# Odd layer's block inverses: PE turns in place of the products that make the transposes, blocks laid home by token tile

## The reference

```python
def rwkv7_scan(r, logw, k, v, kk, a, s0):
    def step(s, inp):
        r_t, lw_t, k_t, v_t, kk_t, a_t = inp
        sa = jnp.einsum('bhvk,bhk->bhv', s, -kk_t)
        s = (s * jnp.exp(lw_t)[:, :, None, :] + sa[..., None] * (kk_t * a_t)[:, :, None, :]
             + v_t[..., None] * k_t[:, :, None, :])
        return s, jnp.einsum('bhvk,bhk->bhv', s, r_t)
```

## Time and profile before

| | us |
|---|---|
| median of 3 runs | 1579.1 (1577.63 to 1582.22) |
| profiled execution | 1576.2, its span 1574.3 |
| PE busy in the span | 1487.2 (94%) |
| DVE, ACT busy | 545.6 (35%), 296.3 (19%) |
| odd layer's blocks 0 to 7, z of block 0 to solve of block 7 | 604.02 to 792.21 |
| experts, to the end | the last 700 or so |

### The profile page before, as it was taken

One profiled execution on the slowest core, in us unless ns is written; L12 is line 12 of the kernel. 1 busy time (PEld: TensorE's weight loads), 2 busy tenths in 40 slices (PEclk: granted clock), 3 DMA queues, 4 the chain that ended last, 5 costly groups with the idle time before them and its releaser, 6 DMA issues.

```text
span 1574.3 us, 62507 instructions
## 1 busy us (share of the span) xinstructions
PE 1487.2 (94%) x28005; PEld 1323.4 (84%) x28005; DVE 545.6 (35%) x1410; ACT 296.3 (19%) x817; POOL 16.4 (1%) x32
## 2 busy tenths in 40 slices
PE   5999888999998999999887999999999999999995
PEld 3888477999546787888866999999999999999995
DVE  1463435666636344666843301010101011010102
ACT  2112423010102432444324101010101010010101
POOL 0100000000000000000000000000000000000000
PEclk9999998999998999999998999999999999999998
DMA  9722676444448144000132799999999999999993
GB/s 391 292 82 100 250 300 270 161 174 181 182 167 314 40 162 150 6 8 8 33 151 81 300 417 379 416 386 418 384 412 409 387 419 380 418 376 417 376 418 131
DMA packets 72895, 407.07 MB, mean 259 GB/s; under 512 B 10514, under 2 KB 10948, under 8 KB 35908
## 3 DMA queue, kind: packets, MB, share of 16 engines
q1 hardware_dynamic: 68176, 398.92, 64.0%
q0 software_dynamic: 1184, 3.41, 0.7%
q10 hardware_dynamic: 3412, 2.93, 0.6%
HBM read 403.31 MB, written 1.92 MB: 257 GB/s over the span
## 4 chain that ended last, share of the span: by engine, by line
PE 37%; PEld 10%; DVE 1%; ACT 1%; issue 1%; PEldq 0%; DVEq 0%; POOL 0%; ACTq 0%
PE bank L1466 20%; PE bank L1486 10%; PEld bank L1466 7%; PEld bank L1486 3%; PE bank L644 2%; PE bank L1448 1%; PE bank L1432 1%; PE bank L1442 0%; PEld bank L1432 0%; PE bank L709 0%; PE bank L1267 0%; PEld bank L1448 0%; DVE w L2036 0%; DVE w L2675 0%; PE bank L1290 0%
## 5 line engine op out<-in xcount | busy, mean ns | idle before, releaser
L1466 PE MATMUL bank<-w,ring 128*64 128x86 f32 x11264 | 452.6, 237 | 1.1 <-ACT w L1959 0.6
L1466 PEld LDWEIGHTS bank<-w,ring 128*64 128x64 f32 x11264 | 432.4, 136 | 9.7 <-issue 8.8
L1486 PE MATMUL bank<-w,ring 128*64 128x86 f32 x5632 | 238.7, 237 | 0.0
L2860 DVE TENSOR_TENSOR w<-w,bank 128x86 f32<-128x86 f32 x176 | 43.1, 245 | 549.0 <-PE bank L1466 541.6
L1486 PEld LDWEIGHTS bank<-w,ring 128*64 128x64 f32 x5632 | 220.8, 137 | 0.0
L1971 ACT ACTIVATE w<-bank 128x86 f32<-128x86 f32 x176 | 42.8, 243 | 572.4 <-PE bank L1466 572.4
L641 PE MATMUL bank<-w,ring 128*128 128x256 f32 x256 | 59.1, 394 | 4.3 <-DVE w L2454 3.7
L641 PEld LDWEIGHTS bank<-w,ring 128*128 128x128 f32 x256 | 50.5, 198 | 13.0 <-DVE w L2454 4.0
L644 PE MATMUL bank<-ring,w 128*128 128x256 f32 x256 | 56.0, 380 | 1.9 <-DVE w L2036 1.9
L644 PEld LDWEIGHTS bank<-ring,w 128*128 128x128 f32 x256 | 48.4, 190 | 8.8 <-DVE w L2036 2.3
L667 PE MATMUL bank<-ring,ct 128*32 128x256 f32 x768 | 47.0, 396 | 2.4 <-ACT ct L1569 2.1
(11 more groups left out here) (437 smaller groups left out, 1795.9 us busy)
## 6 DMA issues: line engine op xcount, KB each, us to landing
ring<-in_moe_gu SPq DMA_DIRECT2D x176, 1024.0 KB, 8.5
ring<-in_moe_w_down SPq DMA_DIRECT2D x176, 512.0 KB, 8.6
ring<-in_ada_w SPq DMA_DIRECT2D x48, 1024.0 KB, 5.0
ring<-in_ev_w_in SPq DMA_DIRECT2D x11, 1024.0 KB, 26.6
ring<-in_ffn_w_gate SPq DMA_DIRECT2D x11, 1024.0 KB, 7.9
ring<-in_ffn_w_up SPq DMA_DIRECT2D x11, 1024.0 KB, 5.2
ring<-in_ffn_w_down SPq DMA_DIRECT2D x11, 1024.0 KB, 6.4
ring<-in_ev_w_out SPq DMA_DIRECT2D x4, 1024.0 KB, 11.0
```

Source lines behind the costliest of these rows:

```text
L1466: ins = [mm(b[hp, 0:CAP], w[:, k, hp], XG[:, k, :], start=k == 0, stop=k == KC - 1, skip_group_check=True) for hp in HALVES]
L1486: ins = [mm(bank[4 + c // 4][hp, (c % 4) * CAP:(c % 4 + 1) * CAP], w[:, c * P + hp.start:c * P + hp.stop], HIDU[:, t % 2, :], start=t == 0 ...
L2860: v.tensor_tensor(HIDU[:, t % 2, :], SILU[:, t % 2, :], bank[2 + t % 2][:, 0:CAP], ALU.mult).then_inc(sem("hid"), 1)
```

## The change

The second part of xp goes at levels 1 to 4. In its place PE turns the new X, four turns of 128x128 into bank 2 (turned_x), and ACT copies the needed columns into IP (take_turned). At level 5 the product stays (last_p), with DVE's masked copy behind it (last_wider). turned_start is four turns as well. For a turn to give what is wanted, the blocks are laid so that the two token tiles lie on the two halves of the partitions (P, z) or the two heads do (X): z writes half j // 2 and reads both, new_x reads half j // 2 and writes both. wider makes four copies of half the size. right_side, solve and carry follow the new layout, and take_right is one copy instead of two. The eight PSUM banks become one tensor with views.

The order changes on each engine: on PE t4(i, 2), t4(i, 3), turned_keys, t4(i + 1, 0) and right_side come earlier, last_states now stands behind right_side and waits for ACT's copies of level 5; on DVE masked(i, 2) stands ahead of wider(i, 1); on ACT take_turned stands ahead of each take_z, the decays are split.

```diff
-        bank = [ctx.enter_context(nc.psum_tensor(f"bank{i}", [P, 512], F32)) for i in range(8)]
+        banks = ctx.enter_context(nc.psum_tensor("banks", [P, 4096], F32))
+        bank = [banks[:, i * 512:(i + 1) * 512] for i in range(8)]
...
-        IP = [tiles4(HTf[:, 512 * k:512 * k + 512]) for k in range(2)]
-        IX, IZ = tiles4(HTf[:, 1024:1536]), tiles4(HTf[:, 1536:2048])
-        GS = tiles4(GBf[:, 0:512])
+        IP = [HTf[:, 512 * k:512 * k + 512].rearrange("p (d a h n) -> p d a h n", d=2, a=2, h=2) for k in range(2)]
+        IX, IZ = HTf[:, 1024:1536].rearrange("p (d a b n) -> p d a b n", d=2, a=2, b=2), tiles4(HTf[:, 1536:2048])
+        GS = GBf[:, 0:512].rearrange("p (r d a n) -> p r d a n", r=2, d=2, a=2)
...
+        def four(lo):
+
+            return banks[:, lo * 512:(lo + 2) * 512].rearrange("p (g n) -> p g n", g=4)
+
+        def state_bank(i):
+
+            return bank[1 if i + 1 < KC else 7]
...
-                    pe.wait_ge(sem("zc"), 10 * i - 1 + d)
-                for j in range(4):
-                    for hp in HALVES:
-                        at = home(d, hp)
-                        ins = mm(bank[2 + d][hp, j * DH:(j + 1) * DH], IP[i % 2][at, d, j, :], ID2[at, :], start=True, stop=True)
-                        if j == 3:
-                            ins.then_inc(sem("z"), 1)
+                    pe.wait_ge(sem("zc"), 18 * i)
+                for a in range(2):
+                    at = (2 * d + a) * P
+                    ins = tr(bank[3][:, at:at + P], IP[i % 2][:, d, a, :, :].rearrange("p h n -> p (h n)"), ident)
+                ins.then_inc(sem("z"), 2)
 
             def z(i, lv):
 
                 if lv == 1:
                     pe.wait_ge(sem("x0"), 2 * i + 2)
                     pe.wait_ge(sem("m4"), 4 * i + 2)
-                    if i:
-                        pe.wait_ge(sem("inv"), 10 * i)
+                    if i >= 2:
+                        pe.wait_ge(sem("so"), i - 1)
                 else:
                     pe.wait_ge(sem("ix"), 8 * i + 2 * (lv - 1))
                 for j in range(4):
+                    to = HALVES[j // 2]
                     for d in range(2):
-                        for hp in HALVES:
-                            ins = mm(z_bank(lv, d)[home(d, hp), j * DH:(j + 1) * DH], M4[i % 2][0][hp, j, 0, queries(d, hp), :],
-                                     IX[hp, d, j, :],
+                        at = (j % 2) * 256 + d * DH
+                        for h, hp in enumerate(HALVES):
+                            ins = mm(bank[h][to, at:at + DH], M4[i % 2][0][hp, j, 0, queries(d, hp), :],
+                                     IX[hp, d, j % 2, j // 2, :],
                                      start=True, stop=True)
                             if j == 3:
                                 ins.then_inc(sem("z"), 1)
 
-            def xp(i, lv):
-                pe.wait_ge(sem("zc"), 10 * i + 2 * lv)
-                if lv > 1:
-                    pe.wait_ge(sem("inv"), 10 * i + 2 * (lv - 1))
-                if lv < 5:
-                    for j in range(4):
-                        for d in range(2):
-                            for hp in HALVES:
-                                at = home(d, hp)
-                                ins = mm(z_bank(lv + 1, d)[hp, j * DH:(j + 1) * DH], IP[i % 2][at, d, j, :], IZ[at, d, j, :],
+            def new_x(i, lv):
+
+                if lv == 1:
+                    pe.wait_ge(sem("zc"), 18 * i + 2)
+                    if i:
+                        pe.wait_ge(sem("inv"), 2 * i)
+                else:
+                    pe.wait_ge(sem("zc"), 18 * i + 4 * lv - 2)
+                for j in range(4):
+                    st, a = j // 2, j % 2
+                    for d in range(2):
+                        at = a * 256 + d * DH
+                        for h, hp in enumerate(HALVES):
+                            ins = mm(bank[2 + st][hp, at:at + DH], IP[i % 2][HALVES[st], d, a, h, :], IZ[HALVES[st], d, 2 * h + a, :],
+                                     start=True, stop=True)
+                            if j == 3:
+                                ins.then_inc(sem("nx"), 1)
+
+            def turned_x(i, lv):
+
+                pe.wait_ge(sem("ix"), 8 * i + 2 * lv)
+                for d in range(2):
+                    for a in range(2):
+                        at = (2 * d + a) * P
+                        ins = tr(bank[2][:, at:at + P], IX[:, d, a, :, :].rearrange("p b n -> p (b n)"), ident)
+                    ins.then_inc(sem("np"), 1)
+
+            def last_p(i):
+
+                pe.wait_ge(sem("zc"), 18 * i + 18)
+                for d in range(2):
+                    for a in range(2):
+                        for h in range(2):
+                            at = (4 * d + 2 * a + h) * DH
+                            for to in HALVES:
+                                ins = mm(bank[2][to, at:at + DH], IZ[to, d, 2 * h + a, :], IP[i % 2][to, d, a, h, :],
                                          start=True, stop=True)
-                                if j == 3:
-                                    ins.then_inc(sem("nx"), 1)
-                for d in range(2):
-                    for j in range(4):
-                        for hp in HALVES:
-                            ins = mm(z_bank(lv, 0)[hp, (4 * d + j) * DH:(4 * d + j + 1) * DH], IZ[hp, d, j, :], IP[i % 2][hp, d, j, :],
-                                     start=True, stop=True)
-                            if d == 1 and j == 3:
-                                ins.then_inc(sem("np"), 1)
+                                if (d, a, h) == (1, 1, 1):
+                                    ins.then_inc(sem("np"), 1)
...
             def last_states(i):
                 pe.wait_ge(sem("trk"), i + 1)
-                pe.wait_ge(sem("y_copy"), i + 1)
+                if i + 1 < KC:
+                    pe.wait_ge(sem("zc"), 18 * (i + 2))
+                else:
+                    pe.wait_ge(sem("y_copy"), i + 1)
                 for h in range(2):
                     for m in range(2):
...
-                    t4(i, 2)
-                xp(i, 1)
+                    t4(i, 3)
+                new_x(i, 1)
                 if i:
                     carry(i - 1)
+                turned_x(i, 1)
                 z(i, 2)
                 if i == 0:
                     half_v(3, 1)
                 else:
-                    t4(i, 3)
-                xp(i, 2)
+                    turned_keys(i - 1)
+                new_x(i, 2)
                 if i:
                     solve(i - 1, 1)
+                turned_x(i, 2)
                 z(i, 3)
                 if i == 0:
                     pe.wait_ge(sem("v_copied"), 3)
                     ada_part(11, 0)
-                else:
-                    turned_keys(i - 1)
-                xp(i, 3)
+                if more:
+                    t4(i + 1, 0)
+                new_x(i, 3)
                 if i:
                     outputs(i - 1)
+                turned_x(i, 3)
                 z(i, 4)
                 if i == 0:
                     ada_part(11, 1)
                 if more:
-                    t4(i + 1, 0)
-                xp(i, 4)
-                z(i, 5)
-                if more:
                     t4(i + 1, 1)
-                xp(i, 5)
+                new_x(i, 4)
                 if i == 0:
                     turn_mods(11)
                 else:
+                    right_side(i)
+                turned_x(i, 4)
+                z(i, 5)
+                if i:
                     last_states(i - 1)
-                right_side(i)
+                last_p(i)
+                if i == 0:
+                    right_side(0)
                 if more:
                     for d in range(2):
                         turned_start(i + 1, d)
+                    t4(i + 1, 2)
                 solve(i, 0)
...
-                    act.wait_ge(sem("z"), 24 * i + 4 * lv + 2 * d + 2)
-                    A(sided(IZ[:, d, :, :], lv, d), sided(z_bank(lv, d)[:, 0:256].rearrange("p (j n) -> p j n", j=4), lv, d),
+                    act.wait_ge(sem("z"), 24 * i + 4 * lv + 4)
+                    A(sided(IZ[:, d, :, :], lv, d), sided(four(0)[:, :, d * DH:(d + 1) * DH], lv, d), ACT.Copy).then_inc(sem("zc"), 1)
+
+            def take_turned(i, lv):
+                for d in range(2):
+                    act.wait_ge(sem("np"), 10 * i + 2 * lv)
+                    A(sided(IP[i % 2][:, d, :, :, :].rearrange("p a h n -> p (a h) n"), lv, 1 - d),
+                      sided(bank[2][:, d * 256:(d + 1) * 256].rearrange("p (g n) -> p g n", g=4), lv, 1 - d),
                       ACT.Copy).then_inc(sem("zc"), 1)
...
                 take_z(i, 1)
+                if more:
+                    decays(i + 1, 0)
                 if i:
                     take_right(i - 1, 1)
+                take_turned(i, 1)
                 take_z(i, 2)
                 if i == 0:
                     take_v(3)
                 if more:
```

(35 more changed lines are left out.)

120 lines of the change are left out of this document (60 added, 60 removed).

## The result

The changed kernel takes 1606.7 us, median of 4 runs (1604.6 to 1611.47); the kernel before, run beside it, 1580.24 (4 runs, 1577.63 to 1582.22). The ratio is 1.0173, with a 95% interval of 1.0145 to 1.0201: 23 to 32 us slower. The prediction had the sign, but said 1590.5 with an upper end of 1602. The profiled execution of the changed kernel took 1606.6, its span 1604.8, which is 30.5 more than the span before.

A forecast was written before the change was run, and what follows sets the result against it. It took spacing of PE's short products and PE's waits to decide. Blocks 1 to 6 +7.6, block 0 +2.4, block 7 +3.9, tail -0.4 sum to +13.5 us; it said 1590.5, range 1577 to 1602.

The forecast's parts named there:

- Part 4: One odd-layer block laid out with its copies, masks and waits: about 24.1 us, +1.27, times six +7.6 us.
- Part 1: PE in a block: four of five L1201 groups go, 3.7 us; the start's 32 instructions become four turns.
- Part 2: Four turns on PE take 0.53 us to the next group; four sets 2.1 us a block, the start's 0.5.
- Part 3: z and new_x on PE: eight products in a row share two quarters; +0.25 us for nine groups, +2.25 a block.
- the faster: Rival: quarters fill as now despite the order; 2.25 us goes from each block; 1575 less 0.4, or 1571; chance 0.12.
- slower rival: No overlap at the quarter switch and DMA issues of 2.05: block 25.3, ends +9, total 1602 us; chance 0.12.
- look ahead: PE starts later products while two quarters are busy: about six instructions, 0.17 us, taken as 0.15 off each group.
- Part 5: First and last blocks and tail: block 0 +2.4 us, block 7 +3.9, tail one ACT copy of 0.4 less.
- clock rival: More PE waits in block 7 could bring the lower clock forward: 2 to 8 us, 1595; chance 0.08.

The follow-up runs named there:

- the kernel before with two quarters: Kernel before, with z and the first part of xp issued direction by direction, so eight products in a row share two quarters: 1584.28 us, ratio 1.0014.

## Why the prediction was right and where it failed

**What failed: Part 4, level 3.** "At level 3, t4(i+1, 0) and new_x 3 to 11.2, outputs to 13.75, which cover the copies; turn 13.85, z4 14.4." The outputs do not cover the copies, because masked(i + 1, 0), which waits for the outputs, stands ahead of the copies on DVE. Part 4 named masked(i, 2) as a DVE instruction that came forward, looked at what stood in front of *it*, and priced it well. It didn't do the same for masked(i + 1, 0), whose place the shown pieces of the order didn't cover, and whose wait costs nothing where it was before. Its price was 1.86 a block; moving the one line gave 12.2 in six blocks, and a period that is 0.38 from the forecast. The diff shown ahead of the prediction did have the line going away from its old place behind `wider(i, 4)`; the question of where it went would have led to it.

The forecast of blocks 1 to 6 was +7.6, the measurement +22.1. The gap of 14.5 is 12.2 for this wait (in it 1.4 of a stretch at half clock in block 2, below), and 6 times 0.38, 2.3, for small errors: z4 to z5 4.93 for 4.7, and the waits at block ends. What is left without the wait agrees: the run with the mask moved is 0.91%, 14.4 us, above the kernel before, where the sum had 13.5. By parts it agrees less well, block 0 1.95, blocks 1 to 6 9.9, block 7 5.1 and the tail -2.4, for 2.4, 7.6, 3.9 and -0.4.

**Part 1, what is removed:** PE's work was forecast to grow by about 0.4 a block, all terms together. Its busy time in blocks 1 to 6 rose by 5.8, from 129.00 to 134.83, 0.97 a block; 1.4 of it is block 2's stretch at half clock, the rest isn't split up. The prediction's "PE waits 2 us a block even now" is a misreading of the earlier trace rows, where it is 7.96 in six, 1.33, and over half of that pauses that ended on nothing the profile shows.

**Part 2, the turns:** right. Four take 0.66, z follows 0.58 after the first (forecast 0.53), and the price of doubling them is 0.37 to 0.42 for four.

**Part 3, home by token tile:** right in size. Groups are 0.97 long where 0.95 was forecast (0.69 and 1.10 would have spoken for the faster and the slower rival), and undoing the order gave back 0.25 a group wherever the group was on the path, 1.63 a block for the 2.25 forecast. The look ahead of the earlier trace rows, which tells 0.97 from 1.10, held. The Trainium skill (TensorE: Matmul & The Clock Gate, What overlaps and what doesn't) states that matmuls start and end in program order. For the starts the rows again show otherwise: in the kernel before with two quarters L1201 starts at 650.01, ahead of three of L1194 at 650.06. On the ends they can't decide, since the profile models them. What I didn't see is that the spread was avoidable: the layout asks for the quarters it uses, but not for their order in time.

**Part 4, the rest of a block:** the copies, 0.61 for 0.65 forecast, 0.72 at level 1 for 0.9. Level 1, masked ahead of the copies and t4 ahead of new x: 4.33 for 4.6, and the cause is shown by moving t4. The block's end, where ACT's issues delay the right side's copy: 4.97 for 5.0. This is DVE at the end of block 4: L2627 (last_wider), the scans and sums, then masked(5, 2), just as Part 4 had them.

```profile
739.88 0.50 DVE L2627 COPY_PREDICATED ht<-msk,banks 128x128 f32<-128x128 uint8 x2 [1.71 <-PE banks L1221]
...
741.84 1.01 DVE L2591 TENSOR_TENSOR ring<-banks,cst 128x384 f32<-128x384 f32 x2
```

**Part 5, the ends:** block 0 +2.17, forecast +2.4. The nearness is partly luck: the terms given, 2.4 for late turns and 2.2 for spread groups less 1.5 to 2, add up to 2.6 to 3.1. Measured, levels 1 to 4 are 1.07, 1.19, 2.07 and 0.14 longer and the end of the block 2.30 shorter; in the kernel before the last two levels held pauses of 0.81 and 1.41 without a releaser. Block 7 +6.37, forecast +3.9. The mechanism is the one named: reduction and addition ahead of the mask, and PE waiting 2.67 for it.

```profile
792.81 1.75 DVE L2680 TENSOR_REDUCE sm<-w 128x24 f32<-128x1536 f32 x1
794.59 2.29 DVE L2676 TENSOR_TENSOR w<-w 128x2048 f32<-128x2048 f32 x1
796.92 1.02 DVE L2591 TENSOR_TENSOR ring<-banks,cst 128x384 f32<-128x384 f32 x2
```

```profile
794.44 0.98 PE L1180 MATMUL banks<-ht,ring 64*64 64x64 f32 x32
798.09 0.69 PE L1148 MATMUL banks<-ring 64*64 64x256 f32 x2 [2.67 <-DVE ring L2591]
```

The first level took 8.44, where 4.6 and 2.4 were forecast, and the second 4.90 for 4.3. Both levels lie in a stretch at the lower clock, 797.3 to 804.2, so the 2.0 in excess fit the **clock** rival, priced at 2 to 8 us. The run with the mask moved bears this out: its edit doesn't touch block 7, which there has 3.4 us at the lower clock (784.0 to 787.4) in place of 6.9 and is 26.99 long in place of 28.22. Its second level, 788.19 to 792.55, has the upper clock throughout and takes 4.36, as forecast; its first, with the 3.4, takes 7.75. What the first would take at the upper clock alone is not shown. The view of stretches for the two places in this stage where the clock fell:

```profile
677.90:681.30 3.40, 3.40 (x76) 3.35 (x72) 0.00 (x0) 0.93 (x5) 0.00 (x0) 0.50 0.00 0
797.30:804.20 6.90, 5.75 (x100) 5.11 (x100) 3.78 (x9) 0.84 (x3) 0.00 (x0) 0.51 0.01 2
```

The tail was forecast 0.4 shorter and is 2.38 shorter up to the output projection. In the kernel before some 3.5 us of it had the lower clock (to about 800.4, the 0.85 of the earlier trace rows); now it has the upper clock throughout, and the lower one comes earlier, in block 7, as the clock rival had it. What that is worth here a later run shows: with each turn behind z, the tail, which that edit doesn't touch, has 3.3 us at the lower clock (796.3 to 799.6) and takes 9.38 in place of 7.84. So about 1.5 of the 2.38 is the clock and about 0.8 the new order, for the 0.4 forecast.

**The range.** Its upper end, 1602, came from the slower rival: no overlap in the quarters, long issues, ends +9. The first two did not happen: groups are 0.97 and not 1.10, and the pair of issues took 1.26 to 1.80. The ends did come to +8.5, in part by the clock. What carried the time past 1602 is a wait that stood in no rival. The sum's own bounds, 22.5 to 25.2 a block, took in the sizes of the waits that were seen and left nothing for one that was overlooked, though the change reorders three engines.
